# Laying out silu(c) to the partitions: six small broadcast transfers in place of six products by spread identities

## The chip, the cores and the metric

The kernel runs on one core of a Trainium2 chip. The metric is the device time of one execution, in microseconds (us), as the median of several runs. The engines are TensorE (PE in the profile, its weight loads PEld), VectorE (DVE), ScalarE (ACT), GpSimd (POOL) and SyncE (SP), which here issues nearly all transfers.

## The reference

Two blocks of a transformer stand one behind the other, all in float32, with 256 tokens of width 2048. The first (two layers) has latent attention with rotary positions, a short gated convolution, attention to 256 memory tokens, a gate and an output product. The second has a Fourier mixer and an MLP of hidden width 8192, both modulated by a vector c. What the change touches is this modulation alone:

```python
silu_c = jax.nn.silu(c)
sh1, sc1, g1, sh2, sc2, g2 = jnp.split((silu_c @ w_mod[i] + b_mod[i])[:, None, :], N_MOD, axis=-1)
```

c has 2048 elements and w_mod is 2048 x 12288, so it's one row times a 100 MB matrix.

## The kernel before, in words

Products are made to float32 accuracy from rounded parts: each piece of weights (a "step", 128 x 1024 elements; two steps are a "unit" of 1 MB, one load) is rounded to `whi` by ScalarE (`split_hi`, line 452), its remainder is made into `wlo` by VectorE (`split_lo`, line 459), and TensorE makes three products per tile (high by high, high by low, low by high). SyncE loads units in order into a ring of four; from unit 4 on, `load_unit` waits until TensorE is through with the unit four before. ScalarE and VectorE each run through a loop over the steps `s`, in which they prepare step s + 3 (`AHEAD`) and then do whatever else is put at s by hand-made tables. Every engine executes its queue in order, so what waits holds up all that stands behind it.

The first 16 steps are the keys and values of the memory (`mem`, units 0 to 7: units 0, 2, 4, 6 are w_mk, the others w_mv), from memory tiles that ScalarE rounds (`round_mem`) and VectorE completes (`mem_rest`). From step 14 on TensorE also turns the normalised x, two tiles a step (line 1658); the turn of tile f from f = 4 on waits until VectorE is through with tile f - 4 (`x_lo`, line 1383). VectorE makes the angles of the rotary positions at steps 6 and 8 (`ANG_AT`), ScalarE squares the two halves of x at steps 6 and 8 (`X_SQ_AT`).

Silu(c) @ w_mod isn't made by TensorE but by VectorE, in 192 units of 128 x 1024 (`mod_unit`, lines 1148 and 1151) from step 18 on. Partition p of unit j holds part of row n of w_mod, where n = j P/groups + p // groups (`groups` is 4 or 2 by pass), so the scalar of partition p must be silu(c) at that row. This is the table `cvx`, one column per unit. It is made like this (`CV_AT`, steps 4, 5, 9, 10): c is loaded with the partition as fast index into `cv` (line 615, 128 x 16), ScalarE makes exp(-c) at step 4 (line 875), VectorE makes 1 + it, its reciprocal and the product with c at step 5 (lines 1297, 1299 and `tt`), the sums `sel` of the identity (line 1304; they are used at the end of each pass) and `alike`, the identity with its columns repeated (line 1305). At step 9 TensorE multiplies with `alike` six times, which spreads the values; the trace shows each as two matmuls, since they are float32. At step 10 ScalarE copies the result to `cvx` (line 878).

The order of the transfers around it (lines 603 to 622): unit 3, memory tiles 12 to 15, `ident`, `cv`, `ropev`, `pos`, `modT`, `ngs`, unit 4, first half of x, unit 5, second half of x, unit 6, unit 7.

```python
                            if l == 0 and i in (4, 5):
                                t = i - 4
                                sp.dma_start(X[:, t, :], x[t * P:(t + 1) * P, :]).then_inc(x_in[t], 16)
```

Of the kernel before, what the change touches and what calls it, by code (L numbers as in the profile page):

```python
# [9 lines left out]
ALU = mybir.AluOpType  # L10
ACT = mybir.ActivationFunctionType
AX_X = mybir.AxisListType.X

P = 128
# [195 lines left out]
assert len(MOD_AT) == MOD_UNITS and len(MOD_SUM) == len(MOD_PASS)  # L210
MOD_END = {c: step for step, c in MOD_SUM.items()}

CV_AT = (4, 5, 9, 10)

ANG_AT = (6, 8, 12, 15)

# [32 lines left out]
def build_program(nc, x, memt, positions, small, w_in, w_uq, w_ukv, w_mk, w_mv, w_o, post_g,  # L249
# [3 lines left out]
    with ctx:  # L253
# [80 lines left out]
        sel = at("sel", [P, 8], m + 0.53125)  # L334
        gs = at("gs", [P, G_CONST], m + 0.5625)

        alike = at("alike", [P, 6 * P], A + 50)
        modT = at("modT", [P, NMOD * KT], m + 0.8125)
        ngs = at("ngs", [P, 4 * KT], m + 1.1875)
        R = at("R", [P, 2 * KT], m + 1.4375)  # L340
        A1 = at("A1", [P, KT], m + 1.5625)
        S1 = at("S1", [P, KT], m + 1.625)
        A2 = at("A2", [P, KT], m + 1.6875)
        cv = at("cv", [P, 3 * KT], m + 1.75)
        ropev = at("ropev", [P, 2], m + 1.9375)
        sc = at("sc", [P, 96], m + 1.96875)
        SS, MS, RS = 0, 4, 8
# [53 lines left out]
            "csx_ready", "ab_ps", "ab_out", "ab_val", "ab_two", "f_ps", "f_pq", "f_mix", "f_hi", "f_lo"))  # L401
        x2_xn, x2_T, x2_val, x2_hi, x2_lo = map(sem, ("x2_xn", "x2_T", "x2_val", "x2_hi", "x2_lo"))
        x_copied, x_sum, conv_in, conv_out = map(sem, ("x_copied", "x_sum", "conv_in", "conv_out"))
        sel_set, cv_T, cv_ready = sem("sel_set"), sem("cv_T"), sem("cv_ready")
        x2_T0, x2_T1, x2_hi0, x2_lo0 = map(sem, ("x2_T0", "x2_T1", "x2_hi0", "x2_lo0"))
        first_hi, first_lo = sem("first_hi"), sem("first_lo")
        mem_first = [sem(f"mem_first{i}") for i in range(3)]
# [161 lines left out]
        def _(sp):  # L569
# [26 lines left out]
            for l in range(DEPTH):  # L596
# [3 lines left out]
                for g, (name, kind, width, units, nk) in enumerate(GROUPS):  # L600
                    for i in range(units):
                        at_unit = UNIT_AT[g] + i
                        u = l * LU + at_unit
                        if kind == "MEM":
                            if u == 2:
                                for j in range(2):
                                    sp.dma_start(raw[2][:, 1024 * j:1024 * (j + 1)].rearrange("p (k n) -> p k n", k=2),
                                                 weight_rows(w_mk[0], 4 + 2 * j, 2, 0, 512)).then_inc((third_in, raw_in[2])[j], 16)
                            elif u > 1:
                                load_unit(sp, u, slot(u, nk, width), weight_rows(mem_w[i % 2][l], i // 2 * nk, nk, 0, width))  # L610
                            if l == 0 and 1 <= i < 4:
                                load_memx(i)
                            if l == 0 and i == 3:
                                sp.dma_start(ident[:, :], consts).then_inc(ident_in, 16)
                                sp.dma_start(cv[:, 0:KT], cvec).then_inc(c_in, 16)
                                sp.dma_start(ropev[:, :], rope_c).then_inc(rope_in, 16)
                                sp.dma_start(pos[:, :], positions.partition_broadcast(P)).then_inc(rope_in, 16)
                                sp.dma_start(modT[:, :], bmod).then_inc(vec_in, 16)
                                sp.dma_start(ngs[:, :], ng2).then_inc(vec_in, 16)
                            if l == 0 and i in (4, 5):  # L620
                                t = i - 4
                                sp.dma_start(X[:, t, :], x[t * P:(t + 1) * P, :]).then_inc(x_in[t], 16)
                            if l and at_unit in (2, 4):
                                b = at_unit // 2 + 1
                                sp.wait_ge(mem_lo, l * KT + 4 * (b - 1))
                                load_mem(b)
                        else:
                            w, c0 = src[name]
                            if name == "gate":
                                of = g - G_OF[name]  # L630
                                c0 = C_GATE + (2 * GATE_PART[of // 2] + of % 2 - of) * width
                            load_unit(sp, u, slot(u, nk, width),
                                      weight_rows(w, i * nk, nk, c0 + (g - G_OF[name]) * width, width))
                        load_mods(2 * u - MOD_LEAD)
# [80 lines left out]
        def _(act):  # L715
# [146 lines left out]
            for l in range(DEPTH):  # L862
                base = l * LH
                for s in range(LH):
# [6 lines left out]
                        nc.scalar.activation(sinT[:, :], ang[:, 0, :], ACT.Sin).then_inc(sin_ready, 1)  # L871
                        nc.scalar.activation(cosT[:, :], ang[:, 1, :], ACT.Sin).then_inc(sin_ready, 1)
                    if l == 0 and s == CV_AT[0]:
                        act.wait_ge(c_in, 16)
                        nc.scalar.activation(cv[:, KT:2 * KT], cv[:, 0:KT], ACT.Exp, scale=-1.0).then_inc(c_exp, 1)
                    if l == 0 and s == CV_AT[3]:
                        act.wait_ge(cv_T, 1)
                        nc.scalar.activation(cvx[:, :], M[2][:, 0:96], ACT.Copy).then_inc(cv_ready, 1)
                    for f in MEM_AT:
                        if s == MEM_AT[f]:  # L880
                            round_mem(l, f)
# [190 lines left out]
        def _(dve):  # L1072
# [62 lines left out]
            def mod_unit(at_step):  # L1135
# [2 lines left out]
                c = pass_of(j)  # L1138
                _, groups, j0 = MOD_PASS[c]
                dve.wait_ge(mod_in[j % MRING], 16 * (j // MRING + 1))  # L1140
                co = (0 if groups == 4 else 64) + j - j0
                co = cvx[:, co:co + 1]
                if j == 0:
                    dve.wait_ge(cv_ready, 1)
                if j == j0:
                    if c:
                        dve.wait_ge(mod_T, c)
# [140 lines left out]
            for l in range(DEPTH):  # L1288
                base = l * LH
                for s in range(LH):  # L1290
# [3 lines left out]
                    if l == 0 and s == CV_AT[1]:  # L1294

                        dve.wait_ge(c_exp, 1)
                        nc.vector.tensor_scalar(cv[:, KT:2 * KT], cv[:, KT:2 * KT], 1.0, None, ALU.add).then_inc(cv_step, 1)
                        dve.wait_ge(cv_step, 1)
                        nc.vector.reciprocal(cv[:, 2 * KT:], cv[:, KT:2 * KT]).then_inc(cv_step, 1)
                        dve.wait_ge(cv_step, 2)  # L1300
                        tt(cv[:, 2 * KT:], cv[:, 2 * KT:], cv[:, 0:KT], ALU.mult).then_inc(cv_step, 1)
                        dve.wait_ge(ident_in, 16)
                        for e0, groups in ((0, 4), (4, 2)):
                            nc.vector.tensor_reduce(sel[:, e0:e0 + groups], ident[:, :].rearrange("p (i e) -> p e i", e=groups), AX_X, ALU.add)
                            w = nc.vector.tensor_copy(alike[:, P * e0:P * (e0 + groups)].rearrange("p (i e) -> p i e", e=groups),
                                                      ident[:, :].unsqueeze(2).broadcast_to([P, P, groups]))
                        w.then_inc(sel_set, 1)
                        dve.wait_ge(vec_in, 32)
                    if base + s + AHEAD < stage_end(base + s):
# [259 lines left out]
        def _(pe):  # L1569
# [55 lines left out]
            for l in range(DEPTH):  # L1625
                base = l * LH
                for s in range(LH if l + 1 < DEPTH else LH - 8):
                    if l == 0 and s == MSUM_AT:
# [2 lines left out]
                        for t in range(MT):  # L1631
                            i = mm(M[0][:, t:t + 1], msq[:, 0, t * P:(t + 1) * P], ones[:, 0:1], True, True)
                        i.then_inc(mem_sum, 1)
                    if l == 0 and s == CV_AT[2]:

                        pe.wait_ge(cv_step, 3)
                        pe.wait_ge(sel_set, 1)
                        for c0, e0, groups in ((0, 0, 4), (64, 4, 2)):
                            for j in range(groups):
                                i = mm(M[2][:, c0 + j:c0 + groups * KT:groups], alike[:, (e0 + j) * P:(e0 + j + 1) * P],  # L1640
                                       cv[:, 2 * KT:], True, True)
                        i.then_inc(cv_T, 1)
                    if l == 0 and s == MROW_AT:
                        pe.wait_ge(mem_rot, 1)
                        pe.wait_ge(ident_in, 16)
# [3 lines left out]
                    if X_T_AT[l] <= s < X_T_AT[l] + KT // 2:  # L1649
                        if s == X_T_AT[l]:  # L1650
                            pe.wait_ge(x_xn, 2 * l + 2)
                            pe.wait_ge(cv_ready, 1)
                            sums_read(base + s)
                        for f in (2 * (s - X_T_AT[l]), 2 * (s - X_T_AT[l]) + 1):
                            if f >= 4:
# [320 lines left out]
```

## Time and profile before

| what | value |
|---|---|
| median of 3 runs | 1675.72 us (1674.74 to 1676.18) |
| the profiled execution's own time | 1674.83 us |
| its span, first to last instruction | 1673.0 us |
| TensorE busy | 1660.2 us, 99% of the span |
| VectorE busy | 1192.8 us, 71% |
| ScalarE busy | 857.6 us, 51% |
| transfers | 408.15 MB, 244 GB/s over the span |
| granted TensorE clock | 0.999 of full speed |

Busy times overlap, since the engines run beside each other; a share of 99% says that the others cover nearly all their work under TensorE's. In a timeline, what stands in brackets behind a row is how long the engine was idle before it and what ended that. All rows of timelines are in us from the start of the span. L463 is the helper that records every matmul and L1074 one that records VectorE's two-tensor operations, so go by the tiles that are named.

### The profile page before, as it was taken

How to read it: one execution, taken by the hardware profiler on the slowest of the kernel's cores; microseconds unless marked ns; L12 is line 12 of the kernel's file. 1: busy time of each engine (PE TensorE's matmuls, PEld its weight loads, DVE VectorE, ACT ScalarE, POOL GpSimd, SP SyncE). 2: the span in 40 equal slices, each digit the busy share in tenths (PEclk: the TensorE clock that was granted, in tenths of full speed). 3: DMA queues.
4: the chain of work that ended last, by engine and by line, in shares of the span. 5: the costliest groups of instructions: out<-in, count | busy, mean ns of one | idle time of the engine just before them, and what ended most of it. 6: DMA issues, size and time to landing. Idle time of an engine off the chain costs nothing.

```text
span 1673.0 us, 22311 instructions
## 1 busy us (share of the span) xinstructions
PE 1660.2 (99%) x8956; PEld 1436.1 (86%) x8956; DVE 1192.8 (71%) x1299; ACT 857.6 (51%) x1212; POOL 25.0 (1%) x42
## 2 busy tenths in 40 slices
PE   9999999999999999999999999999999999999997
PEld 8899888888989988888888788888888888888886
DVE  6878778887877877789688578776654556546655
ACT  7668556444646755544464554434434344334442
POOL 0000000000100000000000000000000000000000
PEclk9999999999999999999999999999999999999999
DMA  9688687897778867799649478787655666666563
GB/s 334 204 286 303 220 268 243 318 363 275 243 255 263 284 216 263 229 350 365 224 156 353 144 229 298 285 292 245 185 185 193 196 183 200 211 192 190 188 201 126
DMA packets 218536, 408.15 MB, mean 244 GB/s; under 512 B 9377, under 2 KB 87745, under 8 KB 217665
## 3 DMA queue, kind: packets, MB, share of 16 engines
q1 hardware_dynamic: 217936, 404.58, 71.3%
q10 hardware_dynamic: 496, 2.14, 0.3%
q8 instruction: 71, 1.16, 0.3%
q14 instruction: 33, 0.26, 0.0%
HBM read 404.58 MB, written 2.11 MB: 243 GB/s over the span
## 4 chain that ended last, share of the span: by engine, by line
PE 97%; DMA 1%; issue 1%; ACT 1%; DVE 1%; POOL 0%; DVEq 0%; POOLq 0%; ACTq 0%
PE banks L463 95%; PE banks L1696 1%; DMA raw<-in_w_mk 1%; PE banks L1658 0%; DMA raw<-in_w_in 0%; PE banks L1667 0%; DVE X L1116 0%; DVE X L1565 0%; PE banks L1853 0%; POOL sc L681 0%; ACT whi L452 0%; ACT junk L724 0%; DVE wlo L459 0%; ACT junk L735 0%; ACT swap L821 0%
## 5 line engine op out<-in xcount | busy, mean ns | idle before, releaser
L459 DVE TENSOR_TENSOR wlo<-raw,whi 128x1024 fp32r<-128x1024 f32 (+2 forms) x561 | 663.3, 1189 | 368.7 <-ACT whi L452 365.8
L452 ACT ACTIVATE whi<-raw 128x1024 fp32r<-128x1024 f32 (+2 forms) x561 | 573.0, 1030 | 576.2 <-PE banks L463 521.8
L463 PE MATMUL banks<-H,whi 128*128 128x512 f32 x2048 | 659.9, 398 | 1.0 <-DVE H L1074 0.7
L463 PEld LDWEIGHTS banks<-H,wlo 128*128 128x128 f32 x2048 | 384.9, 188 | 88.5
L463 PE MATMUL banks<-whi,Y 128*128 128x512 f32 x1472 | 455.7, 389 | 0.0
L463 PE MATMUL banks<-H,wlo 128*128 128x256 f32 x2048 | 402.6, 278 | 0.0
L463 PEld LDWEIGHTS banks<-whi,Y 128*128 128x128 f32 x1472 | 276.3, 188 | 57.2
L463 PEld LDWEIGHTS banks<-H,whi 128*128 128x128 f32 x2048 | 317.0, 189 | 2.2 <-issue 0.8
L463 PE MATMUL banks<-wlo,Y 128*128 128x512 f32 x768 | 298.8, 389 | 0.0
L1151 DVE SCALAR_TENSOR_TENSOR modacc<-modw,cvx,modacc 128x1024 f32<-128x1024 f32 x188 | 240.4, 1279 | 17.1 <-DMA modw<-in_w_mod 17.0
L463 PEld LDWEIGHTS banks<-wlo,Y 128*128 128x128 f32 x768 | 144.2, 188 | 30.0
L463 PE MATMUL banks<-whi,H 128*128 128x512 f32 (+1 forms) x480 | 140.5, 371 | 0.1
L463 PEld LDWEIGHTS banks<-whi,H 128*128 128x128 f32 x480 | 87.7, 188 | 14.1 <-issue 0.5
L463 PE MATMUL banks<-wlo,H 128*128 128x512 f32 (+1 forms) x256 | 94.5, 369 | 0.0
L463 PEld LDWEIGHTS banks<-wlo,H 128*128 128x128 f32 x256 | 48.1, 188 | 7.3
L914 ACT ACTIVATE prob<-banks,sc 128x256 f32<-128x256 f32 x48 | 22.3, 470 | 59.2 <-DVE sc L1333 59.2
L1058 ACT ACTIVATE Y<-sqr 128x1024 fp32r<-128x1024 f32 x16 | 17.0, 1061 | 44.4 <-DVE sqr L1534 44.4
L463 PE MATMUL banks<-memh,whi 128*128 128x256 f32 x128 | 35.1, 291 | 1.1 <-DVE wlo L459 1.1
L681 POOL TENSOR_TENSOR sc<-sc 128x1 f32<-128x1 f32 (+1 forms) x18 | 13.2, 733 | 1465.6 <-DVE sc L1561 713.0
L463 PE MATMUL banks<-meml,whi 128*128 128x256 f32 x128 | 34.6, 286 | 0.0
L463 PE MATMUL banks<-memh,wlo 128*128 128x256 f32 x128 | 34.2, 283 | 0.0
L968 ACT ACTIVATE prob<-prob,sc 128x256 f32<-128x256 f32 x48 | 21.8, 502 | 23.1 <-DVE sc L1337 23.1
(225 smaller groups left out, 1341.9 us busy)
## 6 DMA issues: line engine op xcount, KB each, us to landing
modw<-in_w_mod SPq DMA_DIRECT2D x192, 512.0 KB, 6.5
raw<-in_w_in SPq DMA_DIRECT2D x72, 1024.0 KB, 5.4
raw<-in_w_mlp_in SPq DMA_DIRECT2D x64, 1024.0 KB, 5.6
raw<-in_w_mlp_out SPq DMA_DIRECT2D x64, 1024.0 KB, 5.0
raw<-in_w_o SPq DMA_DIRECT2D x32, 1024.0 KB, 6.7
raw<-in_w_fnet SPq DMA_DIRECT2D x16, 1024.0 KB, 6.9
raw<-in_w_mv SPq DMA_DIRECT2D x7, 1024.0 KB, 6.5
raw<-in_w_mk SPq DMA_DIRECT2D x6, 1024.0 KB, 6.0
```

What stands on the lines that cost most here:

```text
L452: nc.scalar.activation(hi_part(step, n), raw[u % RAW][:, (step % 2) * n:(step % 2) * n + n], ACT.Copy).then_inc(hi_ready, 1)
L459: nc.vector.tensor_tensor(wlo[u % RAW][:, part], raw[u % RAW][:, part], hi_part(step, n).bitcast(F32), ALU.subtract).then_inc(lo_ready, 1)
L463: return nc.tensor.matmul(o, a, b, start=start, stop=stop, skip_group_check=True)
L681: nc.gpsimd.tensor_tensor(sc[:, r0:r0 + n], sc[:, m0:m0 + n], sc[:, POW:POW + n], ALU.pow).then_inc(done, 1)
L914: w = nc.scalar.activation(prob[:, b, t, :], M[b][:, t * SEQ:(t + 1) * SEQ], ACT.Exp, scale=scale, bias=sc[:, NM + 2 * b + t:NM + 2 * b + ...
L968: w = nc.scalar.activation(prob[:, b, t, :], prob[:, b, t, :], ACT.Copy, scale=sc[:, RINV + 2 * b + t:RINV + 2 * b + t + 1])
L1058: nc.scalar.activation(Yhi[:, 4 * j:4 * j + 4, :], sqr[:, :, :], ACT.Copy).then_inc(m_hi, 1)
L1151: nc.vector.scalar_tensor_tensor(modacc[:, :], modw[j % MRING][:, :], co, modacc[:, :], ALU.mult, ALU.add).then_inc(mod_used, 1)
L1696: i = nc.tensor.transpose(M[2][:, kt * SEQ + t * P:kt * SEQ + (t + 1) * P], prob[:, b, t, kt * P:(kt + 1) * P], ident[:, :])
```

## The change

`cv`, its transfer, `alike`, the products and the copy go. In their place SyncE issues six transfers of the same 8 KB of c: each fills 16 columns of `c_rows` (128 x 96), with every row of 16 elements repeated on `groups` (4 or 2) neighbouring partitions. Four stand behind the first half of x, ahead of unit 5, and two behind the second half, ahead of unit 6. All six raise one semaphore, `c_in`. ScalarE makes exp(-c) of all 96 columns at step 7 and waits for all six; VectorE makes the other operations at step 9, ahead of its remainder of step 12, and writes silu(c) straight to `cvx`. The column that a unit reads is numbered accordingly.

```diff
--- before.py
+++ after.py
@@ -210,7 +210,7 @@
 assert len(MOD_AT) == MOD_UNITS and len(MOD_SUM) == len(MOD_PASS)
 MOD_END = {c: step for step, c in MOD_SUM.items()}
 
-CV_AT = (4, 5, 9, 10)
+CV_AT = (7, 9)
 
 ANG_AT = (6, 8, 12, 15)
 
@@ -334,14 +334,14 @@
         sel = at("sel", [P, 8], m + 0.53125)
         gs = at("gs", [P, G_CONST], m + 0.5625)
 
-        alike = at("alike", [P, 6 * P], A + 50)
+        c_rows = at("c_rows", [P, 6 * KT], A + 50)
+        c_gate = at("c_gate", [P, 6 * KT], A + 51)
         modT = at("modT", [P, NMOD * KT], m + 0.8125)
         ngs = at("ngs", [P, 4 * KT], m + 1.1875)
         R = at("R", [P, 2 * KT], m + 1.4375)
         A1 = at("A1", [P, KT], m + 1.5625)
         S1 = at("S1", [P, KT], m + 1.625)
         A2 = at("A2", [P, KT], m + 1.6875)
-        cv = at("cv", [P, 3 * KT], m + 1.75)
         ropev = at("ropev", [P, 2], m + 1.9375)
         sc = at("sc", [P, 96], m + 1.96875)
         SS, MS, RS = 0, 4, 8
@@ -401,7 +401,7 @@
             "csx_ready", "ab_ps", "ab_out", "ab_val", "ab_two", "f_ps", "f_pq", "f_mix", "f_hi", "f_lo"))
         x2_xn, x2_T, x2_val, x2_hi, x2_lo = map(sem, ("x2_xn", "x2_T", "x2_val", "x2_hi", "x2_lo"))
         x_copied, x_sum, conv_in, conv_out = map(sem, ("x_copied", "x_sum", "conv_in", "conv_out"))
-        sel_set, cv_T, cv_ready = sem("sel_set"), sem("cv_T"), sem("cv_ready")
+        sel_set = sem("sel_set")
         x2_T0, x2_T1, x2_hi0, x2_lo0 = map(sem, ("x2_T0", "x2_T1", "x2_hi0", "x2_lo0"))
         first_hi, first_lo = sem("first_hi"), sem("first_lo")
         mem_first = [sem(f"mem_first{i}") for i in range(3)]
@@ -612,7 +612,6 @@
                                 load_memx(i)
                             if l == 0 and i == 3:
                                 sp.dma_start(ident[:, :], consts).then_inc(ident_in, 16)
-                                sp.dma_start(cv[:, 0:KT], cvec).then_inc(c_in, 16)
                                 sp.dma_start(ropev[:, :], rope_c).then_inc(rope_in, 16)
                                 sp.dma_start(pos[:, :], positions.partition_broadcast(P)).then_inc(rope_in, 16)
                                 sp.dma_start(modT[:, :], bmod).then_inc(vec_in, 16)
@@ -620,6 +619,11 @@
                             if l == 0 and i in (4, 5):
                                 t = i - 4
                                 sp.dma_start(X[:, t, :], x[t * P:(t + 1) * P, :]).then_inc(x_in[t], 16)
+                                for j in (range(4), range(4, 6))[t]:
+                                    groups, of = (4, j) if j < 4 else (2, j - 4)
+                                    rows_of = cvec[of * P // groups:(of + 1) * P // groups, :]
+                                    sp.dma_start(c_rows[:, j * KT:(j + 1) * KT],
+                                                 rows_of.unsqueeze(1).broadcast_to([P // groups, groups, KT])).then_inc(c_in, 16)
                             if l and at_unit in (2, 4):
                                 b = at_unit // 2 + 1
                                 sp.wait_ge(mem_lo, l * KT + 4 * (b - 1))
@@ -871,11 +875,8 @@
                         nc.scalar.activation(sinT[:, :], ang[:, 0, :], ACT.Sin).then_inc(sin_ready, 1)
                         nc.scalar.activation(cosT[:, :], ang[:, 1, :], ACT.Sin).then_inc(sin_ready, 1)
                     if l == 0 and s == CV_AT[0]:
-                        act.wait_ge(c_in, 16)
-                        nc.scalar.activation(cv[:, KT:2 * KT], cv[:, 0:KT], ACT.Exp, scale=-1.0).then_inc(c_exp, 1)
-                    if l == 0 and s == CV_AT[3]:
-                        act.wait_ge(cv_T, 1)
-                        nc.scalar.activation(cvx[:, :], M[2][:, 0:96], ACT.Copy).then_inc(cv_ready, 1)
+                        act.wait_ge(c_in, 96)
+                        nc.scalar.activation(c_gate[:, :], c_rows[:, :], ACT.Exp, scale=-1.0).then_inc(c_exp, 1)
                     for f in MEM_AT:
                         if s == MEM_AT[f]:
                             round_mem(l, f)
@@ -1138,10 +1139,10 @@
                 c = pass_of(j)
                 _, groups, j0 = MOD_PASS[c]
                 dve.wait_ge(mod_in[j % MRING], 16 * (j // MRING + 1))
-                co = (0 if groups == 4 else 64) + j - j0
+                co = (0 if groups == 4 else 4 * KT) + (j - j0) % groups * KT + (j - j0) // groups
                 co = cvx[:, co:co + 1]
                 if j == 0:
-                    dve.wait_ge(cv_ready, 1)
+                    dve.wait_ge(cv_step, 3)
                 if j == j0:
                     if c:
                         dve.wait_ge(mod_T, c)
@@ -1294,16 +1295,14 @@
                     if l == 0 and s == CV_AT[1]:
 
                         dve.wait_ge(c_exp, 1)
-                        nc.vector.tensor_scalar(cv[:, KT:2 * KT], cv[:, KT:2 * KT], 1.0, None, ALU.add).then_inc(cv_step, 1)
+                        nc.vector.tensor_scalar(c_gate[:, :], c_gate[:, :], 1.0, None, ALU.add).then_inc(cv_step, 1)
                         dve.wait_ge(cv_step, 1)
-                        nc.vector.reciprocal(cv[:, 2 * KT:], cv[:, KT:2 * KT]).then_inc(cv_step, 1)
+                        nc.vector.reciprocal(cvx[:, :], c_gate[:, :]).then_inc(cv_step, 1)
                         dve.wait_ge(cv_step, 2)
-                        tt(cv[:, 2 * KT:], cv[:, 2 * KT:], cv[:, 0:KT], ALU.mult).then_inc(cv_step, 1)
+                        tt(cvx[:, :], cvx[:, :], c_rows[:, :], ALU.mult).then_inc(cv_step, 1)
                         dve.wait_ge(ident_in, 16)
                         for e0, groups in ((0, 4), (4, 2)):
-                            nc.vector.tensor_reduce(sel[:, e0:e0 + groups], ident[:, :].rearrange("p (i e) -> p e i", e=groups), AX_X, ALU.add)
-                            w = nc.vector.tensor_copy(alike[:, P * e0:P * (e0 + groups)].rearrange("p (i e) -> p i e", e=groups),
-                                                      ident[:, :].unsqueeze(2).broadcast_to([P, P, groups]))
+                            w = nc.vector.tensor_reduce(sel[:, e0:e0 + groups], ident[:, :].rearrange("p (i e) -> p e i", e=groups), AX_X, ALU.add)
                         w.then_inc(sel_set, 1)
                         dve.wait_ge(vec_in, 32)
                     if base + s + AHEAD < stage_end(base + s):
@@ -1631,15 +1630,6 @@
                         for t in range(MT):
                             i = mm(M[0][:, t:t + 1], msq[:, 0, t * P:(t + 1) * P], ones[:, 0:1], True, True)
                         i.then_inc(mem_sum, 1)
-                    if l == 0 and s == CV_AT[2]:
-
-                        pe.wait_ge(cv_step, 3)
-                        pe.wait_ge(sel_set, 1)
-                        for c0, e0, groups in ((0, 0, 4), (64, 4, 2)):
-                            for j in range(groups):
-                                i = mm(M[2][:, c0 + j:c0 + groups * KT:groups], alike[:, (e0 + j) * P:(e0 + j + 1) * P],
-                                       cv[:, 2 * KT:], True, True)
-                        i.then_inc(cv_T, 1)
                     if l == 0 and s == MROW_AT:
                         pe.wait_ge(mem_rot, 1)
                         pe.wait_ge(ident_in, 16)
@@ -1649,7 +1639,6 @@
                     if X_T_AT[l] <= s < X_T_AT[l] + KT // 2:
                         if s == X_T_AT[l]:
                             pe.wait_ge(x_xn, 2 * l + 2)
-                            pe.wait_ge(cv_ready, 1)
                             sums_read(base + s)
                         for f in (2 * (s - X_T_AT[l]), 2 * (s - X_T_AT[l]) + 1):
                             if f >= 4:
```

## Rows read from the trace of the kernel before

**Rows 1.** The page: span, and TensorE and its weight loads.
```profile
span 1673.0 us, 22311 instructions
...
PE 1660.2 (99%) x8956; PEld 1436.1 (86%) x8956; DVE 1192.8 (71%) x1299; ACT 857.6 (51%) x1212; POOL 25.0 (1%) x42
```

**Rows 2.** The chain of waits, 0 to 80 us: start, duration (us), what.
```profile
17.65 9.82 DMA raw<-in_w_mk
...
27.49 1.07 ACT whi L452
...
28.66 1.24 DVE wlo L459
...
30.03 18.54 PE banks L463 x132
...
54.97 0.44 PE banks L1658 x4
```

**Rows 3.** Timeline of TensorE, 27 to 49 us: start, duration (us), line, what.
```profile
32.98 1.41 PE L463 MATMUL banks<-cv,alike 128*128 128x16 f32 x12
...
34.44 0.28 PE L463 MATMUL banks<-meml,whi 128*128 128x256 f32 x1
...
42.66 0.28 PE L463 MATMUL banks<-memh,whi 128*128 128x256 f32 x1
```

**Rows 4.** Timeline of ScalarE, 20 to 75 us, same columns.
```profile
24.16 0.22 ACT L875 ACTIVATE cv<-cv 128x16 f32<-128x16 f32 x1 [0.58 <-DMA cv<-in_cvec]
24.28 0.90 ACT L753 ACTIVATE memh<-memx,gs 128x256 fp32r<-128x256 f32 x2
...
35.46 1.89 ACT L718 ACTIVATE junk<-X 128x2048 bf16<-128x2048 f32 x1
...
37.85 1.06 ACT L452 ACTIVATE whi<-raw 128x1024 fp32r<-128x1024 f32 x1 [0.42 <-DMA raw<-in_w_mk]
```

**Rows 5.** Timeline of VectorE, 20 to 75 us, same columns.
```profile
25.92 0.16 DVE L1297 TENSOR_SCALAR cv<-cv 128x16 f32<-128x16 f32 x1
26.12 0.25 DVE L1299 RECIPROCAL cv<-cv 128x16 f32<-128x16 f32 x1
...
36.97 1.80 DVE L1092 SCALAR_TENSOR_TENSOR sinT<-cosT,sinT 128x256 f32<-128x256 f32 x4
...
39.34 1.22 DVE L459 TENSOR_TENSOR wlo<-raw,whi 128x1024 fp32r<-128x1024 f32 x1
...
52.79 0.87 DVE L1383 SCALAR_TENSOR_TENSOR H<-banks,gs,H 128x256 fp32r<-128x256 f32 x2
```

**Rows 6.** VectorE's groups, 39.4 to 58.7: busy, mean ns, and idle before.
```profile
L459 DVE TENSOR_TENSOR wlo<-raw,whi 128x1024 fp32r<-128x1024 f32 x8 | 9.8, 1219 | 0.0
```

**Rows 7.** Windows: engines' busy us, clock, share of the transfer engines, GB/s.
```profile
18.00:20.00 2.00, 2.00 (x19) 2.00 (x19) 1.30 (x2) 0.81 (x1) 0.00 (x0) 1.00 1.07 370
20.00:22.00 2.00, 2.00 (x19) 2.00 (x18) 0.29 (x1) 1.38 (x2) 0.00 (x0) 1.00 1.15 312
```

**Rows 8.** Timeline of SyncE's queue: start and duration of issues.
```profile
12.22 2.36 SPq L614 DMA_DIRECT2D ident<-in_consts  x1
14.62 0.55 SPq L615 DMA_DIRECT2D cv<-in_cvec  x1
...
20.81 2.74 SPq L622 DMA_DIRECT2D X<-in_x  x1
```

**Rows 9.** Transfers issued: count, KB, us from issue to landing (X: second half).
```profile
ident<-in_consts SPq DMA_DIRECT2D x1, 64.0 KB, 11.7
...
cv<-in_cvec SPq DMA_DIRECT2D x1, 8.0 KB, 9.5
...
X<-in_x SPq DMA_DIRECT2D x1, 1024.0 KB, 14.3
```

**Rows 10.** Tile sel: duration ns (min/median/max), first and last start.
```profile
L1304 DVE TENSOR_REDUCE sel<-ident x2: 276/323/370, 26.5 to 27.1; 128x4 f32<-128x128 f32 x1, 128x2 f32<-128x128 f32 x1
```

**Rows 11.** VectorE's groups by form, whole span.
```profile
L1337 DVE RECIPROCAL sc<-sc 128x2 f32<-128x2 f32 x24 | 3.8, 157 | 0.0
```

## The prediction

> **What bounds the kernel now.** I read the page first: TensorE is busy for 99% of a span of 1673.0 us [rows 1], so only what delays or relieves TensorE's own queue counts. The change touches the first 50 us alone, so next came the chain of waits there [rows 2]. The reader is to see that unit 4 of weights (issued at 17.65) lands at 27.47, that ScalarE's rounding (27.49) and VectorE's remainder (28.66) follow at once, and that TensorE starts at 30.03 and then runs on. From one hand to the next takes 1.17 us (ScalarE start to VectorE start) and 1.37 us (VectorE start to TensorE start). Then TensorE's timeline [rows 3]: the products stand at 32.98, between step 8 and step 9, with TensorE busy on both sides, and step 12 starts at 42.66. Then the slack of the helpers for step 12, the point that decides: ScalarE starts its rounding at 37.85 after an idle 0.42 us that unit 6 ended [rows 4], VectorE starts its remainder at 39.34 [rows 5], so TensorE could begin it at 39.34 + 1.37 = 40.7, 2.0 us before it does. From 39.34 to 58.7 VectorE never idles before a remainder [rows 6]. Last the transfers: in this stretch their engines are full (share above 1, 370 GB/s [rows 7]), so landings are set by what is queued ahead, not by the issue.
>
> **The change, part by part.**
>
> *Products removed.* The group lasts 1.41 us [rows 3]. The second matmul of step 9 starts at 34.44; without the group it would follow the first (32.98) by the 0.12 us of its neighbours, at 33.10. So TensorE gets 1.34 us, if nothing stops it afterwards. The 221 ns copy on ScalarE and the waits on it were late for nobody.
>
> *Six transfers in place of one.* Each has 128 rows of 64 B, as the removed one had. Its price p on the landing of what stands behind is not shown for six in a row; two readings bound it. From the landings: the unit matrix lands at 12.22 + 11.7 = 23.92, the vector c behind it at 14.62 + 9.5 = 24.12 [rows 8, 9]: 0.2 us. From the throughput: while four such small transfers pass (512 rows), 312 in place of 370 GB/s is moved for 2 us [rows 7], 0.116 MB less or 0.31 us, so 0.08 each, and 0.02 for its 8 KB: 0.1. I take p = 0.2, because the landing counts for the wait and is set by the slowest of the engines. An upper bound: a row of 64 B costs as much as one of 2 KB. X's second half lands at 20.81 + 14.3 = 35.11 [rows 8, 9] and unit 6 behind it by 37.85 [rows 4]: 2.74 us for 512 rows of 2 KB, so 0.68 us for 128. The low end is 0.1, the high 0.68.
>
> The Trainium skill, DMA: Bandwidth & Descriptors, section Specifications, says that rows under 512 B miss the line rate, because they are written by read-modify-write. By that rule 64 B rows cost more than their bytes, and the trace agrees: 0.2 us for 8 KB against 0.02 by the bytes alone; with bytes alone the sum below would be +1.8 us, with the rule it is what p makes of it.
>
> *Landings.* Unit 4 has one transfer less ahead: 27.47 - p. The first half of X too. Unit 5 has four more: +3p. X's second half: 35.11 + 3p. The last two small ones come behind it: 35.11 + 5p. Unit 6: +5p.
>
> *SP's queue.* A small issue takes 0.55 us [rows 8]. One leaves, six come: the issue of unit 6, after 20.81 + 2.74 = 23.55, moves to 26.3 at worst. Its data land at 37.8, over 11 us later, so the queue never runs dry and this costs nothing. Unit 7 waits for a TensorE step later than that. Without this cover each issue would cost its 0.55.
>
> *ScalarE, step 7.* The exponential moves from step 4 (where ScalarE idled anyway: 0.58 us there, for c [rows 4]) to behind the rounding of step 10, and it waits for all six. Queued behind it are two roundings of memory (tiles 12, 13), the rounding of step 11, the square of X's second half and the rounding of step 12. It starts at 35.11 + 5p + 0.05, the memory roundings 0.12 us later (as from 24.16 to 24.28 [rows 4]), 0.90 us for the pair, overlapping the next by 0.1. The rounding of step 11 thus starts at 36.08 + 5p. VectorE takes its remainder at 37.25 + 5p and is done with it 1.14 us later (39.34 to the next start in its run), at 38.39 + 5p. The angles follow, 39.34 - 36.97 = 2.37 us [rows 5]: 40.76 + 5p. ScalarE has by then done the square (1.89 us [rows 4] plus its read, end near 39.1 + 5p) and about all of step 12's rounding (to 40.5 + 5p); it is no longer the later one.
>
> *VectorE, step 9.* The gate work moves from step 5, where VectorE then waited for unit 4, to just before the remainder of step 12. The three small operations took 26.50 - 25.92 = 0.58 us [rows 5, 10]; at 96 columns instead of 16 the two simple ones gain 80 elements at about 1 ns each (0.08 each), and the reciprocal, 157 ns at 2 columns and 253 ns at 16 [rows 5, 11], 6.9 ns per column, gains 0.55. The two sums for sel are 0.28 + 0.37 [rows 10], 0.5 with overlap. Sum c = 0.58 + 0.16 + 0.55 + 0.5 = 1.8 us. If the reciprocal's slope is that of the others, 1.3; these are its ends. The two copies to alike (gone) save nothing, since VectorE idled behind them.
>
> *Sum.* Remainder of step 12 at 40.76 + 5p + c, 43.56 with p = 0.2 and c = 1.8: 4.22 us later than now. TensorE starts step 12 at 44.93, 2.27 us later than 42.66, while it was itself free at 42.66 - 1.34 - 0.2 = 41.1: a new stall of about 3.8 us in all (some of it already before step 11), in which the 1.34 us of the products vanish. VectorE is late next: it has no idle time, so its results for the second tile of X that step 14 turns (start 52.79 + 0.87 [rows 5]) end at 57.9. TensorE's turn for tile 5 writes to the bank that they read; it stood at 54.97 [rows 2] + half its 0.44 = 55.2. It moves to 57.9: 2.7 us later than now. After that VectorE's lateness falls below TensorE's and TensorE runs on. In short: net = 5p + c - 0.06, so **+2.7 us**. The ends: p = 0.1, c = 1.3 gives +1.7; p = 0.68, c = 1.8 gives +5.1.
>
> The profiled execution took 1674.83 us and would take 1677.5; it lies 0.9 under the median shown, 1675.72. Against the median I forecast **1678.4**. A difference under 0.2% (3.4 us) can't be told from none in this kernel, so this counts as the same.
>
> **The rivals.**
>
> *A, my forecast: ScalarE stands at the exponential for data queued behind X.* For it: the transfers' engines are full, landings keep their order of issue, and c's landing already made ScalarE wait at step 4. Against it: p is read from one pair of landings. +2.7 us, 1678.4.
>
> *B, the small rows come early.* If they overtake X's long rows, ScalarE doesn't wait. Then VectorE's block alone counts: remainder of step 12 at 39.34 + 1.8 = 41.14, TensorE at 42.5, 0.2 us earlier than now: 1675.5. Against it: c landed after the unit matrix and before what was issued later.
>
> *C, no wait and a cheap block.* With c near 1.3 or less TensorE starts step 12 between 41.1 and 42.0: at the best the whole gain of 1.34 + 0.2, 1674.2. This is still the same.
>
> *D, slower: the small transfers are dear.* Its place is the queue between X's second half and unit 6, its price five times p, on the exponential. It decides from 5p + c - 0.06 = 3.4, so from p = 0.33. At the bound of 0.68 it gives +5.1 us, 1680.8. For it: six of the kind in a row, which read the same few rows repeatedly, are not in the trace, and small rows already cut the throughput. Against it: 0.2 and 0.1 are what the trace shows. The skill's rule on rows under 512 B, named above, would act through this rival.
>
> *E, the transfers do nothing bad and the removed matmuls weren't on the path.* Then 0: TensorE's time is given back later by a wait. It lies between B and C.
>
> **How the numbers follow.** A 0.58, B and E 0.14, C 0.10, D 0.18. The predicted time is A's. A's own range, by p from 0.1 to 0.3 and c from 1.3 to 1.9 and by 0.7 us for the scatter of the runs, is 1677 to 1680. For 8 in 10 I add B and most of D: 1675.3 to 1680.8. Slower by over 0.2% (beyond 1679.1): D, and an eighth of A: 0.25. Faster by over 0.2% (below 1672.4): not even C reaches it, 0.02. The same: 0.73.
>
> **What would show it.** Right: ScalarE's exponential on c_gate starts near 36.2, behind an idle time of some 2 us that the transfer of c ended; idle TensorE time before steps 10, 11 and 12, most before 12, with VectorE's remainder as its releaser; step 12 near 44.9; the reciprocal of 128x96 near 0.8 us; unit 4 lands slightly earlier. Wrong: the exponential starts by 34.5 (B or C), or after 37.5 (D); TensorE without a gap between 30 and 50; the reciprocal under 0.4 us; or a time above 1681 or below 1674.

## The result, and the profile after

The changed kernel takes 1678.93 us (median of 22 runs, 1675.68 to 1681.77), the kernel before 1675.30 (22 runs, 1673.47 to 1677.27). The ratio is 1.0024, with a 95% interval from 1.0018 to 1.0029: slower by 3.6 us. The forecast was 1678.4 with a difference of +2.7. So the time was right to 0.5 us, but a part of that is luck: the forecast stood on 1675.72, the median of 3 runs, where 22 runs give 1675.30. That hides 0.4 of the 0.9 us by which the difference was forecast too small. The difference lies beside the 0.2% (3.4 us) that I had called "no difference": 0.24%, with 0.2% inside its interval, so it isn't settled on which side it lies; the far side had 0.25 of the chance. All ratios leave out one slow run, the seventh of the kernel one_load below, which took 2059.08 us at a mean granted clock of 0.751.

The page of the changed kernel, span and busy times:

```profile
span 1676.6 us, 22287 instructions
...
PE 1659.7 (99%) x8944; PEld 1433.7 (86%) x8944; DVE 1193.1 (71%) x1297; ACT 857.5 (51%) x1211; POOL 26.7 (2%) x42
```

The span is 3.6 us longer than in [rows 1], while TensorE has 12 matmuls fewer and is busy for no longer. What was added must be idle time. TensorE's own timeline shows where it is (start, duration, and in brackets the idle time before and what ended it):

```profile
38.52 0.47 PE L463 MATMUL banks<-whi,memh 128*128 128x512 f32 x1 [0.89 <-DVE wlo L459]
...
43.71 0.36 PE L463 MATMUL banks<-memh,whi 128*128 128x256 f32 x1 [2.19 <-DVE wlo L459]
...
55.71 0.39 PE L463 MATMUL banks<-whi,meml 128*128 128x512 f32 x1
56.33 0.83 PE L1647 MATMUL banks<-ident,xn 128*128 128x128 f32 x4 [0.23 <-DVE H L1382]
56.91 0.48 PE L463 MATMUL banks<-whi,H 128*128 128x512 f32 x1
...
72.56 0.60 PE L1647 MATMUL banks<-ident,xn 128*128 128x128 f32 x4
...
150.65 0.50 PE L463 MATMUL banks<-H,whi 128*128 128x512 f32 x1 [1.30 <-ACT kn L835]
```

The same place in the kernel before, at the turn of X:

```profile
54.58 0.39 PE L463 MATMUL banks<-whi,meml 128*128 128x512 f32 x1
54.81 0.60 PE L1658 MATMUL banks<-ident,xn 128*128 128x128 f32 x4
55.17 0.48 PE L463 MATMUL banks<-whi,H 128*128 128x512 f32 x1
```

Three waits are new before 60 us: 0.89 before step 11, 2.19 before step 12 (the step that stood at 42.66 in [rows 3]), and one at the turn of X at 56.33. There the matmuls on both sides start 56.91 - 55.71 = 1.20 us apart, in the kernel before 55.17 - 54.58 = 0.59, so another 0.6. All are ended by VectorE. The wait at 150 us is far from the change; more on it below. Who held VectorE up is to be read from ScalarE's timeline:

```profile
32.04 1.06 ACT L452 ACTIVATE whi<-raw 128x1024 fp32r<-128x1024 f32 x1 [0.89 <-ACT junk L722]
35.08 0.28 ACT L879 ACTIVATE c_gate<-c_rows 128x96 f32<-128x96 f32 x1 [1.98 <-DMA c_rows<-in_cvec]
35.27 0.89 ACT L757 ACTIVATE memh<-memx,gs 128x256 fp32r<-128x256 f32 x2
36.07 1.04 ACT L452 ACTIVATE whi<-raw 128x1024 fp32r<-128x1024 f32 x1
37.02 1.90 ACT L722 ACTIVATE junk<-X 128x2048 bf16<-128x2048 f32 x1
```

ScalarE stands at the exponential for 1.98 us until the last small transfer lands; behind it wait the memory tiles and the rounding of step 11. Then VectorE's timeline:

```profile
37.15 1.23 DVE L459 TENSOR_TENSOR wlo<-raw,whi 128x1024 fp32r<-128x1024 f32 x1 [0.46 <-ACT whi L452]
38.29 1.80 DVE L1093 SCALAR_TENSOR_TENSOR sinT<-cosT,sinT 128x256 f32<-128x256 f32 x4
...
40.66 0.21 DVE L1298 TENSOR_SCALAR c_gate<-c_gate 128x96 f32<-128x96 f32 x1
40.90 0.75 DVE L1300 RECIPROCAL cvx<-c_gate 128x96 f32<-128x96 f32 x1
41.69 0.26 DVE L1075 TENSOR_TENSOR cvx<-cvx,c_rows 128x96 f32<-128x96 f32 x1
41.86 0.57 DVE L1305 TENSOR_REDUCE sel<-ident 128x4 f32<-128x128 f32 x2
42.34 1.22 DVE L459 TENSOR_TENSOR wlo<-raw,whi 128x1024 fp32r<-128x1024 f32 x1
```

The angles follow the late remainder, the block for silu(c) takes 42.34 - 40.66 = 1.68 us, and only then comes the remainder of step 12. ScalarE's rounding of step 12 had been ready since about 40.2. SyncE's queue, for the place of the transfers:

```profile
18.83 3.44 SPq L625 DMA_DIRECT2D c_rows<-in_cvec  x4
...
22.95 2.74 SPq L621 DMA_DIRECT2D X<-in_x  x1
25.73 1.20 SPq L625 DMA_DIRECT2D c_rows<-in_cvec  x2
26.98 0.60 SPq L418 DMA_DIRECT2D raw<-in_w_mk  x1
```

### The profile page after: what moved, and what is told of

It is laid out like the page before. It is cut to its first block, busy times and chain, and to the rows that moved or that the text cites. A ratio compares the mean times of both kernels' runs of the same rounds, so it can differ in the third digit from the quotient of the medians.

```text
span 1676.6 us, 22287 instructions
## 1 busy us (share of the span) xinstructions
PE 1659.7 (99%) x8944; PEld 1433.7 (86%) x8944; DVE 1193.1 (71%) x1297; ACT 857.5 (51%) x1211; POOL 26.7 (2%) x42
## 4 chain that ended last, share of the span: by engine, by line
PE 92%; DVE 2%; DMA 2%; SPq 1%; issue 1%; ACT 1%; POOL 0%; DVEq 0%; POOLq 0%; ACTq 0%
PE banks L463 91%; DMA modw<-in_w_mod 1%; DVE wlo L459 1%; PE banks L1685 1%; DMA c_rows<-in_cvec 1%; PE banks L1647 0%; DVE modacc L1152 0%; SPq L621 0%; SPq L625 0%; SPq L418 0%; DVE msq L1075 0%; SPq L588 0%; PE banks L1656 0%; DVE X L1117 0%; SPq L614 0%
```

## The experiments

Twelve more runs were made: eight other kernels, the changed kernel once more, and three more traces of the kernel before. The start of the kernel scatters by itself: in the four traces of the kernel before, unit 4 lands between 25.8 and 27.5 us. So beside the medians I read one mark in each trace, the start of the last turn of X (72.56 above). In the four traces of before it stands at 70.82, 69.54, 70.52 and 69.12, mean 70.0. "Shift" is the distance to this mean; it scatters by some 0.9 us to either side, and it says nothing of what comes after 72 us.

| kernel | median us | before, same chip | ratio, 95% interval | shift, us |
|---|---|---|---|---|
| changed | 1678.93 | 1675.30 | 1.0024, 1.0018 to 1.0029 | +2.6 |
| a_again | 1678.52 | 1675.13 | 1.0017, 1.0008 to 1.0026 | +2.8 |
| dve_late | 1676.20 | 1675.13 | 1.0005, 0.9996 to 1.0014 | +1.4 |
| act_late | 1676.00 | 1675.13 | 1.0003, 0.9994 to 1.0011 | +0.4 |
| both_late | 1673.88 | 1675.13 | 0.9991, 0.9982 to 1.0000 | -1.0 |
| early | 1674.83 | 1675.18 | 0.9996, 0.9987 to 1.0005 | -0.5 |
| one_load | 1674.52 | 1675.18 | 0.9994, 0.9985 to 1.0003 | -1.4 |
| twelve | 1680.21 | 1675.18 | 1.0028, 1.0019 to 1.0038 | +4.1 |
| delay3 | 1677.01 | 1675.18 | 1.0010, 1.0001 to 1.0018 | +2.2 |
| no_products | 1674.50 | 1675.40 | 0.9994, 0.9985 to 1.0003 | -1.4 |

**The change once more.** No edit.

> The changed kernel once more, for its scatter and a second trace. Theory one (the waits of the first 57 us are the cause): about 1679, +3 to +4 us to the kernel before; ScalarE again idles some 2 us at the exponential, TensorE idles near 0.9 and 2.2 us before steps 10 and 12. If TensorE's 1.3 us wait at 150 us (ended by ScalarE's kn copy) belongs to the change it comes again; if it is chance it is gone or of another size.

It came out at +3.4 us (interval from 1.3 to 4.4), with the same waits: 1.86 us of ScalarE at the exponential, 0.77 and 2.19 us of TensorE. The wait of the 150 us mark came again, 1.37 us.

**Both operations moved to where their engines have time.**

```diff
-CV_AT = (7, 9)
+CV_AT = (10, 17)
-        c_rows = at("c_rows", [P, 6 * KT], A + 50)
-        c_gate = at("c_gate", [P, 6 * KT], A + 51)
+        c_rows = at("c_rows", [P, 6 * KT], A + 10)
+        c_gate = at("c_gate", [P, 6 * KT], A + 11)
```

> Six transfers where the change has them, but the exponential at step 10 (behind the rounding of step 13) and VectorE's block at step 17, where it has slack. Theory one: no wait is left, TensorE keeps the 1.34 us of the products and, as unit 4 has 8 KB less ahead, 0.2: -1.5 us to the kernel before, about 1674. Rival (the six transfers themselves, by what they do to the landings of weights or to the issue queue, cost the time): it stays at +3 to +4.

The same six transfers in the same places, and 4.6 us faster than a_again on the same chip (1673.88 against 1678.52). ScalarE no longer waits:

```profile
39.37 1.05 ACT L452 ACTIVATE whi<-raw 128x1024 fp32r<-128x1024 f32 x1
40.32 0.27 ACT L879 ACTIVATE c_gate<-c_rows 128x96 f32<-128x96 f32 x1
```

No bracket stands behind the exponential. TensorE's timeline has none between 28 and 60 us either; only the turn of X still loses some 0.5 us:

```profile
52.80 0.83 PE L1647 MATMUL banks<-ident,xn 128*128 128x128 f32 x4
```

So the transfers weren't the cost by what they did to the weights; the place of the two operations in their queues was. This is also the best version found: 1.3 us under the kernel before, with an interval that just reaches 1.

**One of the two moved.**

```diff
-CV_AT = (7, 9)
+CV_AT = (7, 17)
```

> Only VectorE's block moved, to step 17; the exponential stays at step 7 behind X's second half. By net = 5p + c - 0.06 with c = 0: +0.9 us to the kernel before; 2.1 to 2.7 us better than the change as made. Rival (the wait of ScalarE alone is the cause): still +3.

```diff
-CV_AT = (7, 9)
+CV_AT = (9, 9)
```

> Only the exponential moved, to step 9 behind the rounding of step 12; VectorE's block stays at step 9 before the remainder of step 12. Theory one: the block alone counts, -0.2 to 0 us to the kernel before. Rival (VectorE's block alone is the cause): +2.

With VectorE's block gone late (the tiles moved as in both_late), TensorE's timeline still shows ScalarE's wait, and little before step 12:

```profile
39.07 0.47 PE L463 MATMUL banks<-whi,memh 128*128 128x512 f32 x1 [0.89 <-DVE wlo L459]
...
42.59 0.35 PE L463 MATMUL banks<-memh,whi 128*128 128x256 f32 x1 [0.51 <-DVE wlo L459]
...
55.20 0.83 PE L1647 MATMUL banks<-ident,xn 128*128 128x128 f32 x4 [0.23 <-DVE H L1382]
```

With the exponential late and the block where it was, the first wait is gone and the second stays:

```profile
28.67 0.36 PE L463 MATMUL banks<-memh,whi 128*128 128x256 f32 x1 [0.22 <-DVE wlo L459]
...
41.52 0.35 PE L463 MATMUL banks<-memh,whi 128*128 128x256 f32 x1 [1.39 <-DVE wlo L459]
...
54.14 0.83 PE L1647 MATMUL banks<-ident,xn 128*128 128x128 f32 x4 [0.23 <-DVE H L1382]
```

Each half removes a part: from +3.4 to +1.1 (dve_late, +0.9 was expected) and to +0.9 us (act_late). Neither alone is the cause. act_late came out at +0.4 in the trace and +0.9 in the median where I expected -0.2 to 0: its rows show 1.39 us before step 12 and, at 54.14, the second wait, on VectorE's results for X, which I had left out for this case.

**The price of the transfers.** First, all six where c's one transfer stood, with the operations back at steps 4 and 5:

```diff
-CV_AT = (7, 9)
+CV_AT = (4, 5)
                                 sp.dma_start(ident[:, :], consts).then_inc(ident_in, 16)
+                                for j in range(6):
+                                    groups, of = (4, j) if j < 4 else (2, j - 4)
...
```

> The six transfers behind the unit matrix, where c's one transfer stood, and the exponential and VectorE's block back at steps 4 and 5. Theory one: both of these lie in time in which the engines wait for unit 4 anyway, so they cost nothing; TensorE keeps 1.34 us, but unit 4 stands behind five more small transfers, 5p = 1.0 us with p = 0.2: -0.3 us to the kernel before, and TensorE's wait before step 8 is near 2 us where it was 1.05. If p is 0.1: -0.8; if p is 0.68: +2.

It took -0.35 us in the median and -0.5 at the mark of 72 us, as expected. But the other mark that I had named did not come: TensorE waits 0.65 us before step 8, not near 2. The wait of 1.05 us from which I counted goes with a late landing of unit 4: b_again2 has one of 1.02, with a landing at 27.18, and the two traces of before with earlier landings have none. Unit 4 lands at 27.26 here, inside the scatter of before, so the five more small transfers can't be seen in it. ScalarE's exponential waits for nothing:

```profile
23.69 0.27 ACT L879 ACTIVATE c_gate<-c_rows 128x96 f32<-128x96 f32 x1
23.86 0.89 ACT L757 ACTIVATE memh<-memx,gs 128x256 fp32r<-128x256 f32 x2
27.26 1.06 ACT L452 ACTIVATE whi<-raw 128x1024 fp32r<-128x1024 f32 x1 [2.51 <-DMA raw<-in_w_mk]
```

The execution that was traced took 1678.15 us, though, the longest of the eleven, in spite of its early mark. It lost most of it further on, at the place of the wait near 150 us. TensorE's rows there, and windows (the last three columns are its granted clock, the transfer engines' share and GB/s):

```profile
148.36 0.50 PE L463 MATMUL banks<-H,whi 128*128 128x512 f32 x1 [1.77 <-ACT kn L835]
...
158.41 0.59 PE L463 MATMUL banks<-kn,O 128*128 128x256 f32 x2
```

```profile
148.00:150.00 2.00, 1.64 (x7) 1.43 (x8) 1.98 (x2) 0.66 (x2) 0.00 (x0) 0.78 1.11 360
150.00:152.00 2.00, 2.00 (x8) 1.71 (x7) 1.27 (x2) 2.00 (x3) 0.00 (x0) 0.50 1.05 374
152.00:154.00 2.00, 2.00 (x12) 1.72 (x12) 1.09 (x1) 1.54 (x3) 0.00 (x0) 0.87 1.11 358
```

Behind a wait of 1.77 us the granted clock fell to 0.50, the lower of its two levels (1.2 of 2.4 GHz), for some 3.4 us. The stretch between the two rows took 158.41 - 148.36 = 10.05 us; in the changed kernel's trace, where the clock stayed at 1.00, it took 159.13 - 150.65 = 8.48. The low clock thus cost 1.6 us.

Then one transfer of 128 x 96, from an input that is laid out so beforehand:

```diff
+                                sp.dma_start(c_rows[:, :], cvec).then_inc(c_in, 16)
...
-                        act.wait_ge(c_in, 96)
+                        act.wait_ge(c_in, 16)
```

> c arranged as 128 x 96 already in its input, so that one transfer of 128 rows of 384 B does it, at the place of c's one transfer, with steps 4 and 5. Theory one: only its 40 KB more, 0.1 us, stand ahead of unit 4: -1.2 us to the kernel before (about 1674). Rival (the small transfers don't matter, only places in the queues do): the same as with six in that place.

-0.7 us in the median, -1.4 in the trace: against the six, 0.3 us and 0.9 us better. The direction is that of theory one, but the intervals of the two overlap and the mark scatters by as much, so the rival isn't excluded.

Last, the small transfers doubled:

```diff
+                                    sp.dma_start(c_more[:, j * KT:(j + 1) * KT],
+                                                 rows_of.unsqueeze(1).broadcast_to([P // groups, groups, KT])).then_inc(c_in, 16)
...
-                        act.wait_ge(c_in, 96)
+                        act.wait_ge(c_in, 192)
```

> The change as made, but each small transfer is sent twice (the second into a tile that nobody reads), and the exponential waits for all twelve. Theory one: four more and two more ahead of the last landing, 6p = 1.2 us with p = 0.2: +4.5 to +5 us to the kernel before, the exponential starts 1.2 us later behind X's landing. If the wait is only for X's second half and the small ones are free, it stays at +3.5.

```profile
35.75 0.29 ACT L885 ACTIVATE c_gate<-c_rows 128x96 f32<-128x96 f32 x1 [2.37 <-DMA c_more<-in_cvec]
```

The exponential starts 35.75 - 26.38 = 9.37 us after unit 4's landing, in the changed kernel 35.08 - 26.44 = 8.64. Six more small transfers thus cost 0.73 us, 0.12 each, where I expected 1.2 us in all (a_again and dve_late, with six, have 8.53 and 8.64, so this is clear of the scatter). The time nevertheless rose as forecast, to +5.0 us, and the trace gives a reason that I hadn't named. Windows of this kernel, same columns:

```profile
42.00:44.00 2.00, 0.17 (x1) 0.00 (x0) 1.97 (x5) 2.00 (x3) 0.00 (x0) 1.00 0.38 61
44.00:46.00 2.00, 1.61 (x7) 1.64 (x8) 2.00 (x4) 2.00 (x3) 0.00 (x0) 0.56 0.96 368
46.00:48.00 2.00, 2.00 (x13) 2.00 (x12) 2.00 (x3) 1.97 (x3) 0.00 (x0) 0.58 0.31 118
```

Behind the long wait before step 12 TensorE came back at a granted clock of 0.56 to 0.58 over 4 us, so at the lower of its two levels for most of them, as in early's trace; from 48 us on it's 1.00 again. Its matmuls there:

```profile
44.39 0.55 PE L464 MATMUL banks<-memh,whi 128*128 128x256 f32 x1 [2.23 <-DVE wlo L460]
44.74 0.41 PE L464 MATMUL banks<-meml,whi 128*128 128x256 f32 x1
44.95 0.41 PE L464 MATMUL banks<-memh,wlo 128*128 128x256 f32 x1
...
47.71 0.28 PE L464 MATMUL banks<-memh,whi 128*128 128x256 f32 x1
47.82 0.28 PE L464 MATMUL banks<-meml,whi 128*128 128x256 f32 x1
```

They follow each other by 0.21 us until 47.7 and by 0.12 after it: 15 matmuls with 0.09 us more each, 1.4 us. That is of this one execution, whose 1681.42 us are 1.2 above the median; whether the others had such a fall isn't shown. In this trace the wait at the turn of X is gone in exchange (0.6 us), since TensorE is now the later one.

**TensorE's delay alone.** The kernel before with 25 matmuls more ahead of the products:

```diff
+                        for _ in range(25):
+                            mm(M[3][:, 0:SEQ], warm[:, 0:P], warm[:, :], True, True)
                         pe.wait_ge(cv_step, 3)
```

> The kernel before with 25 more matmuls of 0.12 us on TensorE ahead of the products of step 9 (their result isn't used): a delay of 3.0 us of TensorE alone, with the helpers and the transfers as they were. Theory one (a delay of the first 57 us is carried to the end one for one): +3.0 us. Rival (a shift of TensorE against the transfers brings waits later, as the one at 150 us, or is caught up later): clearly more, +4 and over, or less than 2.

+1.8 us in the median, with an interval from 0.2 to 3.0. In the trace, the last turn stands 72.20 - 28.40 = 43.8 us behind the start of step 8, before 70.82 - 30.03 = 40.8: all of the 3.0 us is there at 72 us. What arrives at the end is between, at best, all of it and a small part; the median doesn't settle it. The trace shows where some of it went: its span is 1674.7 us, 1.5 above the mean of the four of before (1673.2), where the shift at 72 us was 2.2. Near 561 us all four traces of before have a wait of 0.29 to 0.84 us, and this one has none.

**The kernel before, three more traces, and without the products.**

> The kernel before, unchanged, for another trace. All seven traces of kernels without the products show a TensorE wait of 0.8 to 1.8 us near 148 us, ended by ScalarE's kn copy, and the one trace of before shows none. Theory one (that wait is chance of the transfers): it's there in some traces of before as well. Rival (it belongs to the change): it is in none. And unit 4, which landed at 27.47 in the first trace and at 25.8 to 27.3 in all others, lands within those.

> A third trace of the kernel before, with the same two questions as the second: is there a TensorE wait near 148 us, and when does unit 4 land.

> A fourth trace of the kernel before, with the same two questions as the second: is there a TensorE wait near 148 us, and when does unit 4 land.

```diff
-                        act.wait_ge(cv_T, 1)
-                        nc.scalar.activation(cvx[:, :], M[2][:, 0:96], ACT.Copy).then_inc(cv_ready, 1)
+                        act.wait_ge(ident_in, 16)
+                        nc.scalar.activation(cvx[:, :], ident[:, 0:96], ACT.Copy).then_inc(cv_ready, 1)
...
-                        for c0, e0, groups in ((0, 0, 4), (64, 4, 2)):
...
```

> The kernel before without the six products alone; the table cvx is copied from the identity instead, so silu(c) isn't laid out and the modulation has other values, at the same cost. Nothing else is moved. Theory one: TensorE has no other wait there, so all of the 1.34 us comes back: -1.3 us to the kernel before. Rival (the slack is taken by a later wait, as the one at 148 us): 0.

Unit 4 landed at 26.16, 27.18 and 25.76 in the three traces, so the 27.47 on which the prediction rests was the latest of four. The products alone: -1.4 us in the trace, as expected, -0.9 in the median (interval from -2.5 to +0.5). On the wait near 148 us, which TensorE has at the first weights behind the keys (L831 or L835 kn), one of the three traces shows it:

```profile
147.53 0.50 PE L463 MATMUL banks<-H,whi 128*128 128x512 f32 x1 [1.13 <-ACT kn L831]
...
561.35 0.50 PE L463 MATMUL banks<-H,whi 128*128 128x512 f32 x1 [0.78 <-ACT kn L831]
```

So it isn't made by the change. But it's there in all nine traces of kernels without the products (0.80 to 1.77 us) and in one of the five with them (this one; not in the first trace of before, b_again2, b_again3, delay3). Its twin in the second layer, near 561, goes the other way: it is 0.29, 0.78, 0.66 and 0.84 us in the traces of before, and none in seven of the nine. Summed, the two are 0.7 us per trace with the products and 1.4 without. Why TensorE's products at 33 us should have a say in a wait at 148 us no run shows; this stays open.

## Why the prediction was right, and where it wasn't

- **Which wait decides.** Right. ScalarE waited 1.98 us ("some 2 us") at the exponential for the last transfer of c, and both_late, which takes away only the two in-order waits, takes away all of the loss (-1.3 us to the kernel before).
- **The landings.** The exponential was to start at 36.16, 8.9 us behind unit 4's landing (27.27); it started at 35.08, since unit 4 landed at 26.44, so 8.6 us behind it. Put into the prediction's own sum, that makes p about 0.16 (an estimate). X's second half lands at 22.95 + 11.7 = 34.65, so 0.38 for two small transfers and 0.05 for the start, 0.19 each; the twelve transfers say 0.12. All lie inside the bounds and far from the upper one of 0.68 (a small row as dear as one of 2 KB). The Trainium skill, DMA: Bandwidth & Descriptors, section Specifications, gives 512 B as the least transfer for the line rate; the traces agree, with 0.12 to 0.2 us for 8 KB where the bytes alone would take 0.02. Five times that, 0.6 to 1.0 us, is their part in the sum 5p + c - 0.06, where the block c has 1.7.
- **SP's queue.** The four small issues took 3.44 us, 0.86 each and not 0.55, and unit 6 was issued at 26.98 instead of 26.3. It was covered all the same, as said: the rounding of step 12 waits for ScalarE's square of X, not for unit 6.
- **The block on VectorE.** It took 1.68 us against 1.8; the reciprocal of 96 columns took 0.75 us against "near 0.8". Its slope of 6.2 ns per column (752 - 253 over 80) is far from the 1 ns of the others, as the two points of before had shown.
- **Step 12.** Counted from unit 4's landing it starts 43.71 - 26.44 = 17.3 us later; the forecast was 44.93 - 27.27 = 17.7. The wait for X's second tile came too. The first 73 us lost 2.6 to 2.8 us, and 2.7 was forecast.
- **What was wrong: "After that VectorE's lateness falls below TensorE's and TensorE runs on".** This is the step that made the difference 0.9 us too small. The spans of the two traces of the changed kernel are 1676.6 and 1676.9 us, 3.4 and 3.7 above the mean of the four of before (1673.2), while at 72 us the shift is 2.6 and 2.8. So 0.8 to 0.9 us more is lost later, at full clock: in both traces the granted clock is 1.00 up to TensorE's last matmul. The place that both traces show is the first weights behind the keys, a wait of 1.30 and 1.37 us where the traces with the products have 0.2 on average; in the second layer they save the twin wait (0.5 on average) again. The pair thus makes some 0.6. Near 763 us the changed kernel's first trace has another wait of 0.2 us, for VectorE (L1716, tile R); a_again's has none.
- **Whether the clock had a part is open.** In 10 of the 22 runs of the changed kernel the mean granted clock is 0.997 or less; they took 1679.96 us on average, the other 12 took 1678.44, which is still +3.1. Of 80 runs of the kernel before one has 0.997. But this doesn't repeat: of a_again's 11 runs, of the same kernel, only one has 0.997, and it took 1677.47 us against 1678.21 for the other ten; twelve's six such runs took 1679.89 on average, its other four 1680.82. And the two executions in which a fall was seen, twelve's and early's, have 0.998, as has a_again's, without one. Behind TensorE's last matmul every trace has several us at the lower level (0.66 from 1670 to 1675 in the changed kernel's), and they move the third digit as well. So that digit doesn't say whether a run had a fall, and not where.
- **Rival B's sum.** For "no wait of ScalarE, VectorE's block alone" I had -0.2. act_late is that case: +0.4 in its trace. The step left out is the second wait: VectorE is 1.8 us late, and its slack at the turn of tile 5 is 55.2 - 53.66 = 1.5, so +0.3.
- **Where I started from.** The one trace of before was a late one (unit 4). The formula survived, since it counts from the landing, but the 0.2 us credited to unit 4 lies far below the scatter of 1.7 us of that landing, and nobody can say that it was there.

## What to carry to other kernels

An operation that is free in itself isn't free in an in-order queue: ask what stands behind it, and whether its data come through a queue that is full. Here two operations of 0.3 and 1.7 us took 4.6 us more in one place of the schedule than three and eight steps later, with the same transfers, bytes and instructions (a_again against both_late; the two tiles also lie elsewhere there). And when a wait is added to a busy engine, count the slack of the next hand-over as well: the late engine is late for all of its customers, until it has idle time again.

## What was new about the hardware

A wait of TensorE of some 2 us can cost more than its length. Two of the fourteen traces have a stretch at the lower clock level behind such a wait. In twelve's it stood behind 2.23 us (and 1.32 us some 5 us earlier), at 0.56 to 0.58 over 4 us, with matmuls 0.21 us apart instead of 0.12, which is 1.4 us more. In early's it stood behind 1.77 us, with no other wait over 0.3 us in the 80 us before, and cost 1.6 us. It doesn't come each time: behind the two waits of 2.19 us (the changed kernel, a_again) and behind nine waits of 0.80 to 1.52 us at the place of early's, the clock stayed at 1.00. What decides no run shows.

A small transfer with a repeated source (128 rows of 64 B) delayed the landing behind it by 0.12 to 0.2 us while the transfer engines were full. Its issue on SyncE took 0.59 to 0.63 us in early, close to the 0.55 of the plain one [rows 8]; the mean of 0.86 for the four in the changed kernel has two issues of 0.84 and 1.25 us in it. Plain loads in the same stretch have such long issues too (0.99 for unit 5 and 1.61 for X in the kernel before), so the repeated source isn't shown to be the reason.
